# Layer norm with both sums made tile by tile, in a two-layer decoder step on one Trainium2 core

## The reference

```python
mod = silu(c) @ w_ada[l] + b_ada[l]            # 6 vectors of 1024 per sequence
u = x * (1 + sc1) + sh1
m = mixer(u)                                   # gated conv + gated delta rule, output product
x = layer_norm(ALPHA * x + (1 + g1) * m)
u = x * (1 + sc2) + sh2
f = dense_ffn(u)  (layer 0)   or   moe_ffn(u)  (layer 1, top 2 of 8)
x = layer_norm(ALPHA * x + (1 + g2) * f)

def layer_norm(x, g, b):
    mu = mean(x);  xc = x - mu
    return xc * rsqrt(mean(xc * xc) + 1e-5) * g + b
```

## Time and profile before

| | |
|---|---|
| runs | 1349.72 us median (1347.95 to 1352.23) |
| span of the profiled execution | 1347.1 us; its own run time isn't recorded, the runs lie 0.9 to 5.1 us above the span |
| PE busy | 1296.2 us, 96% |
| DVE, ACT, POOL busy | 857.1, 582.9, 54.3 us |
| first layer norm, in the trace | 246 to 273 us |
| second | 479 to 497 us |
| third | 696 to 720 us |

### The profile page before, as it was taken

One profiled execution on the slowest core, in us unless ns is written; L12 is line 12 of the kernel. 1 busy time (PEld: TensorE's weight loads), 2 busy tenths in 40 slices (PEclk: granted clock), 3 DMA queues, 4 the chain that ended last, 5 costly groups with the idle time before them and its releaser, 6 DMA issues. The chain is left out here.

```text
span 1347.1 us, 24949 instructions
## 1 busy us (share of the span) xinstructions
PE 1296.2 (96%) x10594; PEld 1091.4 (81%) x10594; DVE 857.1 (64%) x1346; ACT 582.9 (43%) x751; POOL 54.3 (4%) x104
## 2 busy tenths in 40 slices
PE   7999899999999999989999999999999999999996
PEld 3667797799999967669877999999867787876673
DVE  2678558555444457865767544644555769999896
ACT  1352334353342325334424433333335556777762
POOL 7000030000000000002100000000000000000000
PEclk8999999999999999989999999999999999999998
DMA  9666645955544553556442835634656779999990
GB/s 318 230 229 233 234 150 188 327 157 157 166 163 155 174 162 102 212 164 220 134 127 70 259 102 161 215 122 150 207 187 206 223 245 296 343 339 352 342 340 36
DMA packets 190038, 276.07 MB, mean 205 GB/s; under 512 B 7845, under 2 KB 136127, under 8 KB 184808
## 3 DMA queue, kind: packets, MB, share of 16 engines
q1 hardware_dynamic: 177856, 263.62, 58.7%
q10 hardware_dynamic: 12072, 10.86, 2.8%
HBM read 268.16 MB, written 6.30 MB: 204 GB/s over the span
## 5 line engine op out<-in xcount | busy, mean ns | idle before, releaser
L823 DVE TENSOR_TENSOR lo_raw<-raw,hi 128x2048 fp32r<-128x2048 f32 (+2 forms) x112 | 229.4, 2056 | 99.7 <-ACT hi L1933 61.0
L1933 ACT ACTIVATE hi<-raw 128x2048 fp32r<-128x2048 f32 (+2 forms) x112 | 193.6, 1728 | 113.6 <-PE bank L1095 78.2
L1063 PE MATMUL bank<-UH,hi 128*128 128x288 f32 x704 | 209.3, 297 | 0.3 <-DVE lo L2384 0.3
L1065 PE MATMUL bank<-UL,hi 128*128 128x288 f32 x704 | 207.0, 294 | 0.0
L2384 DVE TENSOR_TENSOR lo<-raw,hi 128x2048 fp32r<-128x2048 f32 (+1 forms) x42 | 95.8, 2282 | 85.6 <-ACT hi L2169 48.5
L1064 PE MATMUL bank<-UH,lo_raw 128*128 128x288 f32 x496 | 147.2, 297 | 0.0
L1063 PEld LDWEIGHTS bank<-UH,hi 128*128 128x128 f32 x704 | 132.0, 188 | 0.9 <-DVE lo L2384 0.6
L1065 PEld LDWEIGHTS bank<-UL,hi 128*128 128x128 f32 x704 | 132.5, 188 | 0.0
L1064 PE MATMUL bank<-UH,lo 128*128 128x288 f32 x432 | 127.4, 295 | 0.0
L1093 PE MATMUL bank<-hi,UGH 128*128 128x512 f32 (+9 forms) x288 | 111.7, 388 | 0.0
L1095 PE MATMUL bank<-hi,UGL 128*128 128x512 f32 (+9 forms) x288 | 107.9, 375 | 0.0
(11 more groups left out here) (497 smaller groups left out, 2690.4 us busy)
## 6 DMA issues: line engine op xcount, KB each, us to landing
raw<-in_w_ada_dram SPq DMA_DIRECT2D x48, 1024.0 KB, 7.5
raw<-in_w_in_dram SPq DMA_DIRECT2D x28, 1024.0 KB, 8.3
raw<-in_w_exp_gate_dram SPq DMA_DIRECT2D x26, 1024.0 KB, 5.9
raw<-in_w_exp_up_dram SPq DMA_DIRECT2D x26, 1024.0 KB, 7.8
raw<-in_w_exp_down_dram SPq DMA_DIRECT2D x16, 1024.0 KB, 5.2
raw<-in_w_exp_down_dram SPq DMA_DIRECT2D x16, 768.0 KB, 4.6
raw<-in_w_ff_gate_dram SPq DMA_DIRECT2D x11, 1024.0 KB, 5.5
raw<-in_w_ff_up_dram SPq DMA_DIRECT2D x11, 1024.0 KB, 5.4
```

The lines of the kernel that those rows point to most:

```text
L823: dve.tensor_tensor(lo_x[g % XRAW][:, 0:XG[g][2] * XG[g][3]], x_raw(g), hi_x[g % XSPLIT][:, 0:XG[g][2] * XG[g][3]].bitcast(F32), ALU.subtr ...
L1063: pe.matmul(out, wh, xh, start=start, stop=False)
L1065: return pe.matmul(out, wh, xl, start=False, stop=stop)
L1933: act.activation(hi_x[q][:, 0:XG[g][2] * XG[g][3]], x_raw(g), ACT.Copy).then_inc(S("x_hi_made"), 1)
```

## The change

**The sums.** `mean_part` and the step `lnv` are gone. GpSimd adds tiles 0 to 5 of `xT` into one tile of `XSUM`, and their squares, which ACT makes from the tiles before they are centred, into another (`sum_pair`). PE sums three tiles for the mean (`XSUM`, tile 6, tile 7) and three for the squares. The variance is the mean of the squares less the square of the mean.

```diff
+            def sum_pair(which, q):
+                for x, src in enumerate((xT, XSQ)):
+                    if x == 1:
+                        pool.wait_ge(S("x_squared"), 5 * which + q + 1)
+                    for d in ((2 * q, 2 * q + 1) if q else (1,)):
+                        op = pool.tensor_tensor(XSUM[:, x, :], src[:, 0, :] if d == 1 else XSUM[:, x, :], src[:, d, :], ALU.add)
...
+                    pe.wait_ge(S("norm_pool"), norm_count(POOL_DOES, which, "sum"))
+                    sum_part(0, XSUM[:, 0, :], first=True)
...
+                    sum_part(0, xT[:, 6, :])
+                    pe.wait_ge(S("x_added"), (1, 3, 4)[which])
+                    sum_part(0, xT[:, 7, :], last=True).then_inc(full[6], 1)
...
+                    sum_part(1, XSUM[:, 1, :], first=True)
...
+                    dve.scalar_tensor_tensor(LNR[:, :], bank[7][:, 0:N], 1.0 / D, MSQ[:, :], ALU.mult,
+                                             ALU.subtract).then_inc(S("norm_dve"), 1)
```

```diff
+DVE_DOES = ("uab", "mean", "centre0", "var", "centre1", "scale0", "centre3", "scale3")
+POOL_DOES = ("sum", "sum_squares", "centre2", "scale1", "scale2")
...
+                            for d in ds:
+                                op = act.activation(U_[:, d, 0:NP_], xT[:, d, 0:NP_], ACT.Identity,
+                                                    bias=UAB[:, 1, d, 0:1], scale=UAB[:, 0, d, 0:1])
```

**First feed-forward weights.** Their high and low parts are made earlier in the list, ahead of the adds of the last output block:

```diff
+                elif k == 'wo':
+                    if s[2] > 0 and s[3] == 0:
+                        if s == ('wo', 0, 3, 0):
+                            act.wait_ge(full[1], base[1])
+                            act.wait_ge(S("nst_stored"), 64)
+                            hi_part(m + 1)
+                        for b in (0, 1):
+                            act.wait_ge(read[b], base[b])
+                        squares(2 * s[2] - 2, 2)
...
                     if k == 'wo':
                         dve.wait_ge(read[5], base[5])
+                        if s == ('wo', 0, 3, 0):
+                            low(SPLITS[m + 1][0], m + 1, 0, 0)
                         got(base, b)
```

**The rest.** `past_in` is issued behind the exponential of the second layer norm instead of ahead of the squares. The last addition of the feed-forward part signals tile 6 before tile 7. The spins of the first layer norm go from 17 and 3 to 5 and 1:

```diff
-                                spin(3, 0, 17 if q == 0 else 3)
+                                spin(3, 0, 5 if q == 0 else 1)
...
+                    act.activation(LNR[:, :], LNR[:, :], ACT.Exp, scale=-0.5).then_inc(S("ln_rstd"), 1)
+                    if s[2] == 1:
                         past_in(l + 1)
```

More of the change, by code:

```diff
@@ L193, in steps_of @@
     s = [('start',), ('params',)]
-    early = [(0, c) for c in range(ADA_CB)] + [(1, c) for c in range(4)]
-    late = [(1, c) for c in range(4, ADA_CB)]
-    ada = list(early)
+    ada = [(l, c) for l in range(DEPTH) for c in range(ADA_CB)]
     last = []
@@ L438, in banks_of @@
     if k == 'lnm':
-        return one(6)
-    if k == 'lnv':
-        return one(7)
+        return one(6, 7)
     return {}
@@ L477, with norm_count, normed @@
         SPLITS += [(_n + 2 * UP_CB + _b, DOWN_K[_b % 3] * 256) for _b in range(12)]
+NORM_POOL = (1, 2)
+DVE_DOES = ("uab", "mean", "centre0", "var", "centre1", "scale0", "centre3", "scale3")
+POOL_DOES = ("sum", "sum_squares", "centre2", "scale1", "scale2")
+ACT_DOES = ("mean_squared", "log")
+def norm_count(does, which, what):
+    return len(does) * which + does.index(what) + 1
+def normed(which, q):
+    if q in NORM_POOL:
+        return "norm_pool", norm_count(POOL_DOES, which, f"scale{q}")
+    return "norm_dve", norm_count(DVE_DOES, which, f"scale{q}")
 F0 = next(p[1] for t, p in zip(STEPS, POS) if t[0] == 'ffn')
@@ L493 @@
 TILE_FULL = {}
+ADDED = {}
 C0_FULL = []
@@ L1140, in rest_due, with sum_part @@
                     rest_block(g + REST_AHEAD)
-            def mean_part(d):
-                return pe.matmul(bank[6][:, 0:N], ones[:, :], xT[:, d, :], start=(d == 0), stop=(d == KT - 1))
+            def sum_part(x, src, first=False, last=False):
+                return pe.matmul(bank[6 + x][:, 0:N], ones[:, :], src, start=first, stop=last)
             def turn_past(l, base):
@@ L1525, in step @@
                     which = 2 * l + s[2]
-                    if s[2] == 0:
[L1527 to L1545, removed]
-                    which = 2 * l + s[2]
-                    fill(base, 7)
-                    for d in range(KT):
-                        if d % 2 == 0:
-                            pe.wait_ge(S("x_squared"), QTR * which + d // 2 + 1)
-                        mm = pe.matmul(bank[7][:, 0:N], ones[:, :], XSQ[:, d, :], start=(d == 0), stop=(d == KT - 1))
-                    mm.then_inc(full[7], 1)
+                    fill(base, 6)
+                    fill(base, 7)
+                    if s[2] == 1:
+                        pe.wait_ge(S("x_added"), 2)
+                    pe.wait_ge(S("norm_pool"), norm_count(POOL_DOES, which, "sum"))
+                    sum_part(0, XSUM[:, 0, :], first=True)
+                    if s[2] == 0:
+                        pe.wait_ge(read[0], base[0])
+                    sum_part(0, xT[:, 6, :])
+                    pe.wait_ge(S("x_added"), (1, 3, 4)[which])
+                    sum_part(0, xT[:, 7, :], last=True).then_inc(full[6], 1)
+                    pe.wait_ge(S("norm_pool"), norm_count(POOL_DOES, which, "sum_squares"))
+                    sum_part(1, XSUM[:, 1, :], first=True)
+                    pe.wait_ge(S("x_squared"), 5 * which + 4)
+                    sum_part(1, XSQ[:, 6, :])
+                    pe.wait_ge(S("x_squared"), 5 * which + 5)
+                    sum_part(1, XSQ[:, 7, :], last=True).then_inc(full[7], 1)
                 elif k == 'ffn':
@@ L1943, in scale_x, with squares @@
                 op.then_inc(S("x_scaled"), 1)
+            def squares(d, n_):
+                act.activation(XSQ[:, d:d + n_, :], xT[:, d:d + n_, :], ACT.Square).then_inc(S("x_squared"), 1)
             def exps():
```

204 lines of the change are left out of this document (137 added, 67 removed).

## The result

The changed kernel takes 1374.01 us (median of four runs, 1368.32 to 1376.40) against 1350.70 us (four runs) of the kernel before: ratio 1.017, 95% interval 1.0152 to 1.0189. It is slower by 23 us, where 1344 was forecast and 1354 was the upper end of the range. The profiled execution spans 1366.6 us; it is the fastest of the four, the others span 1371 to 1375 at a granted clock of 0.972 to 0.974 instead of 0.978. So the trace accounts for 19.5 us, the growth of the span. The other 4 of the median's 23.3 go with the lower granted clock of the other executions; where in the program they lie no trace shows.

A forecast was written before the change was run, and what follows sets the result against it. PE, 96% busy, was taken as the bound, and inside norms the normalising chain. Terms 0.7 - 1.7 - 4.7 - 1.5 + 1.6 = -5.6 us took the span from 1347.1 to 1341.5; adding 2.6 gave 1344 us, range 1334 to 1354.

The forecast's parts named there:

- Slots elsewhere come free long before use: Moved conditioning products outside the norms: their buffer slots were said to be free early, with no cost priced.
- The moved products in layer 0's solve: One product was to fill a place where PE idled 1.47 us: 0 to -3, taken as -1.5 us.
- First norm: Up to the first feed-forward product: 24.9 us instead of 21.7, waiting on a later weights load; net +0.7 us.
- The first two rivals: First feed-forward load lands in 5 us (1337 us in all, chance 0.22) or 14 us (1349 us, chance 0.18).
- Second norm: Between feed-forward and layer 1's next input: 10.4 us instead of 13.6, net -1.7 us, bounds -3.2 and 0.
- at most 2.1 us to land: Second norm: the past rows' load, issued behind the exponential, was to land within 2.1 us, as before.
- Third norm: Ahead of the router's product: 7.8 us instead of 12.9, nothing loaded; net -4.7 us, bounds -6 and -2.
- So the spins end last, not DVE: Third norm: PE's spins were to end at 7.8 us, the next input being ready at 6.6.
- GpSimd beside DVE: All norms: GpSimd's additions and scaling were to be covered by slack or other PE work; cost taken as 0.
- third rival: GpSimd's last additions and scaling end late in the norms: +11.7 us, 1356 us in all, chance 0.12.
- Layer 1's solve: One conditioning product gone, so DVE's chain shows there; 0.3 us given back, +1.6 us.
- The purse: PE's sums in three norms: ten products fewer each at 0.52 us, 5.2 us a norm, 15.6 in all.

The follow-up runs named there:

- x4: Kernel before, norms untouched, with only the changed kernel's order of conditioning products: 1367.59 us against 1348.59.
- z3: `y2` with its one extra conditioning product in layer 0's solve moved from `c0` to ahead of step Y 16: 1355.93 us against 1346.28.
- y1: Changed kernel with the old product order, except one extra product beside `c0` and one product, not two, in the first norm: 1353.44 us.
- x2: Changed kernel with the past rows' load issued at the second norm's start instead of behind its exponential: 1361.51 us.
- y3: `y2` with GpSimd's normalising operations moved to DVE, GpSimd keeping the pre-additions: 1339.00 us.
- z4: `y3` with DVE's first low half put earlier and GpSimd's pre-additions removed, PE summing all eight tiles and squares: 1349.26 us.
- x3: Changed kernel with GpSimd's three normalising operations moved to DVE, GpSimd keeping the additions: 1369.60 us.
- y2: `y1` with the past rows' load also issued at the second norm's start: 1346.28 us.
- z2: `y3` with DVE's first low half put earlier and 17 and 3 spins ahead of the first feed-forward block: 1336.03 us.

## Why the prediction was wrong, point by point

- **"Slots elsewhere come free long before use" is the step that failed.** The moved products in layer 0's solve were priced at -1.5 us, for filling an idle time. That idle time is not in the trace after. But the ring of six slots is filled in order, and I asked only when a product's own slots come free, not which loads stand behind it in SyncE's queue. Measured: +9.0 in the changed kernel, +9.2 by the order alone (`x4`), +10.8 at `cs_out` for one product (`z3`). At 10.5 us it is the largest part of the error of 25 us in the span; the others are 2.3, 4.0 and 2.5 in the three norms, 4.1 in layer 1's solve and 1.7 behind them.
- **First norm: +0.7 forecast, +3.0 in its stretch.** The chain was right up to the exponential: weights asked for at A + 0.07, ACT at work on them 9.45 us later (9.2 forecast for the landing), low part, adds, and PE idle for 7.1 us until the first of them was done. It was 26.6 instead of 24.9 us long (the recorded terms make 24.7), because DVE's input, stretched by GpSimd, and not PE's own products ended it. The halved clock came, but for a shorter time: 0.50 only from 270 to 273. The first two rivals (a landing of 5 or 14 us) fell. That the kernel pays for the load, and that one product less in the norm cures it (`y1`), was seen in part: I had the cause, "the load was moved back in the same edit", and forecast +0.7 us of it.
- **Second norm: -1.7 forecast, +2.3 measured.** The step "at most 2.1 us to land" failed: behind two loads of 1 MB it took 6.6. I had read the load in a place where nothing stood ahead of it, and did not ask what SyncE issues at that time in the new order. `x2` shows the price of the step, 4.4 us.
- **Third norm: -4.7 forecast, -2.2 measured, and 1.7 lost again behind it**, in part at least on the router's slow products. "So the spins end last, not DVE" was wrong: DVE ended 1.9 us later than they did.
- **GpSimd beside DVE: 0 taken.** The rows have 3.5 us of stretching in each norm. In the first norm the 1.2 us of the first operation hid, but for 0.3, behind the slow squares on PE. Repaired it is worth 4 to 7 us (`y3`). Here a rule spoke against the change and was right: the Trainium skill ("SBUF — State Buffer", the section "SBUF: two separate sides") has the two engines lock each other out for whole instructions, and DVE's 0.76 us operation took 1.95 to 2.00 beside one of 1.40 us. The trace agrees: both began together, and DVE's ended 0.6 us behind GpSimd's. My bound from it, one instruction for a norm, was too low too: two or three DVE operations are stretched on each chain. My third rival had the engine right and half of the operations: it priced the scaling at 1.8 us a norm, near the 2.3 that scaling and narrow operation lost, but the 6.3 of its 11.7 us that it put on the pre-additions were not to be found: PE never waited for them.
- **Layer 1's solve: +1.6 forecast, +5.7 in the trace.** The sign was right. Of the size, +3.7 is there with the order alone (`x4`); but this stretch, products taken out, went from -3.2 (`z4`) to +8.4 (`x3`) against before over the kernels here, so it can't be told from one execution. It stays open, and so do the 4 us of the median's growth that the traced execution does not hold.
- **The purse was right:** 36 records, 0.5 us a product, and `z4` gives 4.5 us for each norm for what GpSimd took over (5.2 forecast).

Repaired one by one, the medians go 1374.0 (changed), 1353.4 (order, `y1`), 1346.3 (past rows, `y2`), 1339.0 (normalising on DVE, `y3`), 1336.0 (spins and low half, `z2`). The third step is the least certain of them, as said at `y3`. With its details repaired the kernel is 15 us under the kernel before; the details had cost 38.

## What to carry to other kernels

When a step that loads is moved in a program with a ring of buffers, write out for each load behind it which use frees its slot: an in-order queue passes one late slot on to everything behind it, and one product put next to others in the ring cost 10 us here, of the 15 that the repaired edit gives. A load read as fast is fast for what stood ahead of it; price it again in the new place. And give GpSimd work that has slack (the pre-additions), not work that is to run beside DVE's own half of the same tiles.

## What the runs showed of the hardware

- The narrow DVE operation (128x64) took 1.31 us beside a GpSimd operation of 1.91 us, and 0.22 us without: in this kernel the wait fell on the small DVE instruction as on the large ones.
- GpSimd's 288-wide addition took 0.81 us alone, and two took 3.27 us beside DVE's split of 2.29 us and the adds behind it, in the first norm of the changed kernel; they had slack, and it cost nothing.
- Idle times of like length were followed by slow stretches of unlike length: 7.1 us idle in the first norm, and 3 us at 0.50 (then 0.71 for 3 us, then 1.00); 7.2 of 10 us idle in layer 0's solve, and 0.50 still 6 us after work resumed (then 0.92 from 168 to 174). The windows of the first norm after:

```profile
270.00:273.00 3.00, 2.42 (x4) 1.33 (x5) 2.44 (x15) 0.89 (x2) 1.25 (x2) 0.50 0.90 272
273.00:276.00 3.00, 3.00 (x15) 1.79 (x17) 2.60 (x3) 0.44 (x1) 1.40 (x1) 0.71 0.01 2
276.00:284.00 8.00, 5.80 (x52) 3.28 (x44) 7.05 (x12) 4.35 (x9) 3.28 (x2) 1.00 0.82 260
```
